# Softmax attention on one Trainium2 core: ScalarE copies weighed values and totals out of PSUM, VectorE divides for two heads at once

## What is computed

```python
def forgetting_attention(q, k, v, log_f):       # 8 heads of 64
    F = jnp.cumsum(log_f, axis=1).transpose(0, 2, 1)
    ...
        logits = jnp.einsum('bhqd,bhkd->bhqk', qb, kh) + fq[..., :, None] - F[..., None, :]
        logits = jnp.where(kpos[None, :] <= qpos[:, None], logits, -jnp.inf)
        p = jax.nn.softmax(logits, axis=-1)
        return jnp.einsum('bhqk,bhkd->bhqd', p, vh)
...
    y_mix = jnp.concatenate([rms_norm(y_lru, gn_lru_g[l]), rms_norm(y_fox, gn_fox_g[l])], axis=-1)
    x = x + y_mix @ w_out[l]
    x = x + peer(rms_norm(x, norm2_g[l]), ...)
```

## Time and profile before

| | us |
|---|---|
| median of three runs (2739.37 to 2740.38) | 2739.71 |
| the profiled execution | 2741.34 |
| its span, first to last instruction | 2739.5 |
| busy in the span: PE | 2670.2 |
| DVE | 2323.9 |
| ACT | 1272.3 |
| POOL | 1437.7 |

### The profile page before, as it was taken

How to read it: one execution, slowest core, us unless ns; L and a number is a source line. 1 busy time by engine, 2 the same in 40 slices (tenths; PEclk the granted TensorE clock), 3 DMA queues, 4 the chain that set the end, 5 groups by cost and what they waited for, 6 DMA issues and landing times. The chain is left out here.

```text
span 2739.5 us, 40163 instructions
## 1 busy us (share of the span) xinstructions
PE 2670.2 (97%) x14923; PEld 2362.3 (86%) x14923; DVE 2323.9 (85%) x4158; ACT 1272.3 (46%) x2551; POOL 1437.7 (52%) x937
## 2 busy tenths in 40 slices
PE   7999899989999999999999999999999999999998
PEld 6777566679999999999999999997888888888887
DVE  4297897449989989988989898877999999999997
ACT  4244443233322223998899999863222222222222
POOL 1122321014248886666666666553666666666652
PEclk9999899999999999999999999999999999999999
DMA  4110101233249886999999999999999999999995
GB/s 125 41 39 24 62 1 39 77 99 98 67 154 304 301 297 219 378 391 398 400 388 409 401 390 405 393 389 375 387 388 388 388 388 388 386 387 388 387 386 210
DMA packets 333059, 762.67 MB, mean 278 GB/s; under 512 B 24176, under 2 KB 159344, under 8 KB 330304
## 3 DMA queue, kind: packets, MB, share of 16 engines
q0 software_dynamic: 111104, 403.02, 38.9%
q1 hardware_dynamic: 221040, 353.68, 36.0%
q10 hardware_dynamic: 720, 3.41, 0.3%
HBM read 667.73 MB, written 92.27 MB: 277 GB/s over the span
## 5 line engine op out<-in xcount | busy, mean ns | idle before, releaser
L2144 POOL DMA_INDIRECT v_rows<-in_peer_v,row_numbers x336 | 535.6, 1594 | 328.4 <-DVE y_rest L2217 194.0
L1775 PE MATMUL expert_pre<-h2T,wq_then_uT_hi 128*128 128x320 f32 x4096 | 669.3, 312 | 2.3 <-PEq L1454 2.3
L1889 POOL DMA_INDIRECT u_rows<-in_peer_u,row_numbers x384 | 534.4, 1392 | 241.9 <-DVE row_weights L1909 162.4
L1775 PEld LDWEIGHTS expert_pre<-h2T,wq_then_uT_hi 128*128 128x128 f32 x4096 | 609.4, 188 | 2.4 <-issue 2.4
L2274 PE MATMUL expert_out<-v_hi,w_hi 128*128 128x512 f32 x1280 | 499.8, 390 | 11.9 <-DVE w_lo L2195 11.3
L1909 DVE CUSTOM_DVE_ANT_0 u_rows<-u_rows,h_rows_kept 128x1024 f32<-128x1024 f32 x384 | 487.4, 1297 | 23.5 <-DMA u_rows<-in_peer_u,row_numbers 22.7
L2274 PE MATMUL expert_out<-v_lo,w_hi 128*128 128x512 f32 x1280 | 498.7, 390 | 0.0
L2274 PE MATMUL expert_out<-v_hi,w_lo 128*128 128x512 f32 x1280 | 498.7, 390 | 0.0
L2217 DVE SCALAR_TENSOR_TENSOR y_rest<-v_rows,row_weights,y_rest 128x1024 f32<-128x1024 f32 x256 | 327.3, 1283 | 19.3 <-DMA v_rows<-in_peer_v,row_numbers 18.6
L1775 PE MATMUL expert_pre<-h2T,wq_then_uT_lo 128*128 128x320 f32 x2048 | 342.0, 309 | 0.0
L1775 PEld LDWEIGHTS expert_pre<-h2T,wq_then_uT_lo 128*128 128x128 f32 x2048 | 310.9, 188 | 0.0
(11 more groups left out here) (350 smaller groups left out, 4001.7 us busy)
## 6 DMA issues: line engine op xcount, KB each, us to landing
pick_memory<-in_peer_v SPq DMA_DIRECT2D x128, 512.0 KB, 12.9
wq_then_u<-in_peer_u_turned SPq DMA_DIRECT2D x86, 512.0 KB, 8.2
pick_memory<-acts_dram SPq DMA_DIRECT2D x128, 320.0 KB, 12.3
acts_dram<-expert_acts SPq DMA_DIRECT2D x124, 320.0 KB, 6.1
gates_dram<-pick_memory SPq DMA_DIRECT2D x19, 2048.0 KB, 11.3
pick_memory<-gates_dram SPq DMA_DIRECT2D x58, 448.0 KB, 14.3
third_u<-in_peer_u_turned SPq DMA_DIRECT2D x42, 512.0 KB, 8.3
wq_then_u<-in_peer_wq SPq DMA_DIRECT2D x32, 512.0 KB, 4.0
```

Of the source, the lines that this page charges most:

```text
L1775: last = nc.tensor.matmul(pre[:, (2 * c + half) % 4, 0:WIDTH], part[:, c % 2, k], m.h2T[:, t, k, HALVES[half]], start=n == 0, stop=n == le ...
L1889: pool.indirect_dma_start(rows[:, k % RING], None, table, bass.IndirectOffsetOnAxis(ap=m.row_of[:, f, slot:slot + 1], axis=0)).then_inc(fe ...
L2144: pool.indirect_dma_start(rows[:, k % ROW_RING], None, d.peer_v, bass.IndirectOffsetOnAxis(ap=m.row_of[:, f, slot:slot + 1], axis=0)).then ...
```

## The change

- ScalarE copies the weighed values of each head and half from PSUM to `foxT` (`keep_values`) and the totals to a new SBUF tile `totals` (`keep_totals`), each counted on `mixed_kept`. For half 0 both follow the fifth exponential of the head (after the high parts), for half 1 they follow the first and the second exponential of the next head.
- TensorE's weighings wait for these copies, no longer for VectorE's product.
- VectorE's finish works for a pair of heads: one reciprocal in place and one product of 128x512 for each half. Half 0 follows placing and low parts of the odd head, half 1 stands at the start of the next even head.
- The last weighing of a head goes behind the first key logits of the next.
- The high parts of head h + 2 go behind the fifth exponential, from the third; the squares of head 6 behind the ninth.
- Five probability buffers in place of six.

```diff
-    LOGIT_BANKS, PROBS, SLOTS, HALF0 = 3, 6, 3, 4
-    TURN_AT, FINISH_AT = 8, 0
+    LOGIT_BANKS, PROBS, SLOTS, HALF0 = 3, 5, 3, 4
+    TURN_AT, FINISH_AT, SQUARE_LATE = 8, 0, 8
...
-        inverse = sb("inverse_totals", [P, HALF])
+        totals = sb("totals_of_two_heads", [P, 2, HALF])
...
+        mixed_kept = Counted(m.blocks_zeroed, 2)
...
                     if j == 0:
                         if h:
-                            pe.wait_ge(fox_done, 2 * h - 1 + half)
+                            mixed_kept.wait(pe, 2 * (2 * h - 1 + half))
...
                 for h in range(FH):
                     for i in range(ST):
                         key_logits(h, i)
-                        if i:
-                            weigh(h, i - 1)
+                        if ST * h + i:
+                            weigh(*divmod(ST * h + i - 1, ST))
...
-                    weigh(h, ST - 1)
                     if h == FH - 3:
                         pe.wait_ge(squares_added, nth["lru", CT - 1] + 1)
                         square_sums(squares_sum[:, 0], 0)
+                weigh(FH - 1, ST - 1)
...
                     if kind == "fox":
-                        act.wait_ge(fox_done, 4 * c + 4)
+                        act.wait_ge(fox_done, 2 * c + 2)
...
+                def keep_values(h, half):
+                    here, there = half_rows(h)
+                    act.wait_ge(weighed, ST * h + (HALF0 if half == 0 else ST))
+                    A(foxT[here, h // 2, half * HALF:(half + 1) * HALF], mixed[here, half], ACT.Copy
+                      ).then_inc(mixed_kept.semaphore, 1)
+
+                def keep_totals(h, half):
+                    here, there = half_rows(h)
+                    if h >= 2:
+                        act.wait_ge(fox_done, 2 * (h // 2 - 1) + half + 1)
+                    A(totals[here, half], mixed[there, half], ACT.Copy).then_inc(mixed_kept.semaphore, 1)
...
                 for h in range(FH):
                     for i in range(ST):
                         exp(h, i)
-                        if i == 2 and h >= 1 and h + 2 < FH:
+                        if i == HALF0 and h >= 1 and h + 2 < FH:
                             high(h + 2)
-                        if i == 4:
+                        if i < 2 and h:
+                            (keep_values, keep_totals)[i](h - 1, 1)
+                        if i == HALF0:
+                            keep_values(h, 0)
+                            keep_totals(h, 0)
+                        if i == (SQUARE_LATE if h == FH - 2 else HALF0):
                             for kind, c in after.get(h, []):
                                 square(kind, c)
...
+                keep_values(FH - 1, 1)
+                keep_totals(FH - 1, 1)
                 square("fox", PAIRS - 1)
...
-                def finish(h, half):
-                    dve.wait_ge(weighed, ST * h + (HALF0 if half == 0 else ST))
-                    if 2 * h + half:
-                        dve.wait_ge(fox_done, 2 * h + half)
-                    here, there = half_rows(h)
-                    v.reciprocal(inverse[here], mixed[there, half]).then_inc(inverse_done, 1)
-                    dve.wait_ge(inverse_done, 2 * h + half + 1)
-                    v.tensor_tensor(foxT[here, h // 2, half * HALF:(half + 1) * HALF], mixed[here, half], inverse[here],
-                                    ALU.mult).then_inc(fox_done, 1)
+                def finish(p, half):
+                    mixed_kept.wait(dve, 2 * (2 * (2 * p + 1) + half + 1))
+                    v.reciprocal(totals[:, half], totals[:, half]).then_inc(inverse_done, 1)
+                    dve.wait_ge(inverse_done, 2 * p + half + 1)
+                    of = foxT[:, p, half * HALF:(half + 1) * HALF]
+                    v.tensor_tensor(of, of, totals[:, half], ALU.mult).then_inc(fox_done, 1)
...
                 for h in range(FH):
                     for i in range(ST):
-                        if i == FINISH_AT and h:
-                            finish(h - 1, 1)
+                        if i == FINISH_AT and h and h % 2 == 0:
+                            finish(h // 2 - 1, 1)
                         if h + 1 < FH:
                             top(h + 1, i)
                     if h + 1 < FH:
                         split_tops(h + 1)
-                    finish(h, 0)
                     if h + 1 < FH:
                         place_tops(h + 1)
                     if h >= 1 and h + 2 < FH:
                         low(h + 2)
+                    if h % 2 == 1:
+                        finish(h // 2, 0)
                     for kind, c in after.get(h, []):
                         gain(kind, c)
-                finish(FH - 1, 1)
+                finish(PAIRS - 1, 1)
                 gain("fox", PAIRS - 1)
```

More of the change, by code:

```diff
@@ L146, in project @@
         constant_in = sem("constant_in")
-        zeroed = sem("blocks_zeroed")
+        zeroed = m.blocks_zeroed = sem("blocks_zeroed_then_mixed_kept")
         product_done, product_read = sem("product_done"), sem("product_read")
@@ L654, in attend @@
         fox_done, inverse_done = sem("fox_done"), sem("inverse_done_then_fox_lo")
+        mixed_kept = Counted(m.blocks_zeroed, 2)
         m.w_out_hi_done, m.w_out_lo_done = Counted(f_split, 2), Counted(f_placed, 2)
-        m.w_out_lo_pool, m.fox_hi_done, m.fox_lo_done = Counted(rows_set, 3), Counted(raw_done, FH), Counted(inverse_done, 2 * FH)
+        m.w_out_lo_pool, m.fox_hi_done, m.fox_lo_done = Counted(rows_set, 3), Counted(raw_done, FH), Counted(inverse_done, 2 * PAIRS)
         squared, squares_added = sem("squared"), sem("squares_added")
```

## The result

The changed kernel takes 2750.05 us (median of 6 runs, 2748.87 to 2752.66) where the kernel before takes 2739.41 (6 runs, 2737.74 to 2740.38). The ratio is 1.0038, with a 95% interval of 1.0028 to 1.0049: slower by 10.6 us, where 8.3 were forecast.

The account below looks back on a forecast made before the run. Bound by TensorE (97% busy) then VectorE (85%), but order within a head decides. Heads and stage end sum to +5.95 us, plus 2.4 for the clock, +8.35: 2748.0 us, range 2741 to 2754 (2745 to 2752 without rivals).

Parts of the forecast that it names:

- VectorE's order decides: Even heads: two finishes in a row put the first top 10.19 us after first key logits; TensorE idle some 4.5.
- Odd and even heads: Attention stage: odd heads 19.11 us, even heads 23.79 before the clock's part; heads 1 to 4 together +4.33.
- The clock: Even heads 2, 4, 6: after TensorE's idle stretches the clock falls, costing 0.8 us each, +2.4 in all.
- Head 6: Attention head with square sums for VectorE: first top 8.48 us after first key logits, 22.08 us against 19.40, +2.68.
- Last weighing: Head boundaries: moved behind the next head's first key logits, it saves 0.34 us each; turned tops to key logits becomes 3.16.
- High parts later: ScalarE within a head: the 0.88 us wait goes, first key logits to row logits 4.95 instead of 5.99; Pool's copies covered.
- The signs named ahead: Timeline marks: VectorE idle about 4 us before placing tops; two reciprocals 4.9 apart; TensorE waiting some 4.5; clock under 1.
- Head 7 and the end: Last head and stage end: copies ahead of a wanted exponential cost 0.1 us, copies ahead of the last finish 0.65.
- (a): Rival, attention stage: the clock holds despite TensorE's idle stretches, +5.95 us, 2745.7 us; chance 20%.
- (b): Rival, attention heads: VectorE's total work sets the period, so the saved 32.6 us frees it, -6.6 us, 2733.1 us; chance 11%.
- (d): Rival: ScalarE's copies hold each head's second exponential, or the clock stays low into key logits; up to +14 us, 2754; chance 5%.
- (c): Rival, VectorE's chain before even heads' first top: shorter by some 2 us, total +0 to +1, 2740 us; chance 9%.

Follow-up runs that it names:

- both finishes in the gap: Changed kernel with both finishes of a pair between split and placing of tops, head 6's squares behind the twelfth exponential: 2735.24 us, ratio 0.9983 to the kernel before.
- filled run: Changed kernel plus 18 useless 128x128 matmuls behind the third row logits in heads 2 and 4: 2746.82 us, ratio 1.0026 to the kernel before.
- high parts alone: Kernel before with one edit, the high parts of head h+2 behind the fifth exponential: 2744.00 us, ratio 1.0010.
- one finish in the gap: Changed kernel with the finish of half 0 between split and placing of tops, half 1 left at the even head's start: 2742.57 us, ratio 1.0010 to the kernel before.

## Why the prediction was right, step by step

- **VectorE's order decides.** Right, in kind and size. First top of an even head at 10.34 and 10.35 where 10.19 was worked out; stand of TensorE 4.72 and 4.73 where "some 4.5" was. The run with both finishes in the gap takes this cause away alone and wins 13.4 us of the stage.
- **Odd and even heads.** 18.97 for 19.11. Even heads 25.31 and 25.38 for 23.79 plus 0.8 for the clock. The filled run gives 23.78 and 23.81 without the clock's part. That the walk was off by only 0.02 there is partly luck: the first top came 0.14 later than worked out, and the turned tops lay 0.14 nearer to t0 (3.02 for 3.16).
- **The clock, the term that was mis-sized.** 1.5 and 1.6 per head in heads 2 and 4 instead of 0.8. The prediction bounded it by half of 3.4 us, which is the time at half rate that its two rows from 1850 to 1856 give (twice 0.47 and 0.10 of 3 us), and let VectorE's pace cover part of it. The stretch was about 6.8 us long in heads 2 and 4 (0.51 over 6.90), and the work of 3.2 us from the fourth row logits on takes 6.4 us at half rate, more than VectorE's 5.04: nothing was left to cover. Where the stretch was about 3.4 long, in head 2 of the version with the high parts alone, the fall cost 0.9 (5.91 from first top to sixth key logits), about what was forecast. The rule that the prediction set beside its sum, that each even head pays again, held for heads 2 and 4 and not for head 6.
- **Head 6.** 21.46 for 22.08 + 0.8: first top at 8.01, not 8.48, and no fall of the clock. The chain from the turned tops was 12.9 there and not 13.3: the placing starts 0.31 behind the turned tops, not 0.44, since it no longer waits behind a finish as in the earlier trace rows, the low parts end 0.1 earlier, and finish with gain take 4.65, not 4.87. In heads 2 and 4 Pool gave this back: the product took 1.15 instead of 0.69 beside Pool's copies.
- **Reciprocal of 128x512.** 3.35, as on 64 partitions; product 0.69; copies 0.59 for 0.57. Right.
- **Last weighing.** 0.48 for 0.34 per boundary (3.02 from turned tops to t0). The run with this edit alone shows it, and shows that 0.1 of it is lost again before the row logits: a head won 0.35 to 0.38, so 0.34 was right for the head though not for the boundary.
- **High parts later.** t0 to row logits 4.95 and 4.96 for 4.95. But the prediction said that Pool's copies behind them "stay covered". That was wrong as a general statement: their own lateness is covered, what they hold on VectorE is not. The changed kernel has the same hold, the row at 332.01 with its 1.79 us in head 1 and one like it in head 5. It did no harm there, since VectorE still waits 2.37 us ahead of the placing; alone in the old order it turned the gain into a loss.
- **The signs named ahead.** VectorE waited 3.7 to 4.0 us ahead of the placing, as said, but 2.4 in heads 1 and 5, where Pool had held it. The two reciprocals lie 4.65 apart, not 4.9.
- **Head 7 and the end.** 16.49 instead of 15.92, +0.57 where 0.1 was said; the sixth exponential there waits for two copies, and the weighings behind it move. End 9.90 for 9.14, +0.76 for 0.65.
- **The sum.** Stage: +8.5 measured, +8.35 forecast. That it is so near is luck: heads 1 to 4 came 1.2 above their part of the forecast with its 1.6 for the clock, head 7 and the end 0.6, and head 6 came 1.4 and head 0 0.2 below. The other 2 us of the median lie outside the stage as far as one execution of each can tell; there the clock fell after a wait that both kernels have. For the medians this is argued and not shown.
- **The rivals.** (a), the clock holds, is out by the granted clock of 0.87 and by the filled run. (b), VectorE's total work, is out: the finishes cost nothing or 13 us by their place alone. (d), copies on TensorE's path, holds for head 7 and the end only. (c), a shorter chain, is out: from the turned tops to the first top it took 13.36 in head 2, where 13.35 was worked out, and only head 6 had 0.4 less.

One thing was not seen ahead: that a finish ahead of the first top has to wait for ScalarE's copy of the totals, at t0 + 3.2. It lay hidden in the changed kernel and shows only when the finish of half 0 is moved away, in heads 4 and 6 of that version.

## What to carry to other kernels

When work is halved by pairing, ask where in its engine's queue the remaining half lands: here eight finishes, two of them in a row ahead of each even head's first top, took 13 us more of the stage than the same eight in the gaps where VectorE waits, and the changed stage is 8.5 longer than that with sixteen finishes. Put such work where the engine waits for another one. And read a short idle stretch of TensorE in dense matmul work as more than its length: behind it the clock may fall, and in this kernel 1.8 us of waiting cost up to 2.5 us more.

## What the runs showed of the hardware

- Stands of TensorE of 1.27, 1.79 (three times), 1.85, 2.49, 4.72 and 4.73 us within dense matmul work were each followed by a stretch at 1.2 GHz, while one of 2.48 (head 6 of the changed kernel) and one of 2.28 (the kernel before, at 797) were not. At least three more falls had no such stand before them and came during or just behind square sums, 16 matmuls of one column in 1.8 to 2.1 us: in head 6 with the high parts alone and, after a wait of 0.49, at the stage's end with both finishes in the gap and in the filled version. Behind most such sums the clock held. The waits of up to 0.9 us in the kernel before never brought the clock down in its heads 1 to 6.
- A stretch at 1.2 GHz of about 3.4 us (high parts alone, head 2) cost 0.9 us, one of about 6.8 us 1.5 (the filled comparison) to 2.5 (one finish in the gap, head 2).
- Idle time filled with useless matmuls made heads shorter than leaving it idle: 25.3 to 23.8 us. Where TensorE hadn't stood still, 6 such matmuls cost 0.9 us.
- VectorE's 128x4 operation with two SBUF operands took 1.78 us beside Pool's 128x1024 add and 0.71 beside the rest of a copy, for 0.16 alone, and ended with Pool's instruction each time; its 128x512 product took 1.15 for 0.69 beside Pool's copies.
